# Two feed-forward up-projections computed turned: weight blocks stationary, positions moving

## The reference

```python
# block 1, hidden width 8192
y = jnp.square(jax.nn.relu(h @ w_ff1[l])) @ w_ff2[l]
# block 2, hidden width 5504
def conv_ffn(h, w_up, conv_w, conv_b, w_down):
    S = h.shape[1]
    val, gate = jnp.split(h @ w_up, 2, axis=-1)
    gp = jnp.pad(gate, ((0, 0), (CONV_W - 1, 0), (0, 0)))
    g = conv_b
    for i in range(CONV_W):                    # CONV_W = 3, causal along positions
        g = g + conv_w[i] * gp[:, i:i + S]
    return (jax.nn.silu(g) * val) @ w_down
```

## Time and profile before

| | us |
|---|---|
| median of 3 runs | 2932.68 (2930.49 to 2933.91) |
| the profiled execution, its own time | 2932.17 |
| its span | 2930.4 |
| PE busy in it | 2703.2 (92%), 12554 matmuls |
| PEld busy | 2192.0 (75%) |
| DVE busy | 1818.0 (62%) |
| ACT busy | 1224.4 (42%) |
| mean granted TensorE clock | 0.970 of full speed |

### The profile page before, as it was taken

How to read it: one execution, slowest core, us unless ns; L and a number is a source line. 1 busy time by engine, 2 the same in 40 slices (tenths; PEclk the granted TensorE clock), 3 DMA queues, 4 the chain that set the end, 5 groups by cost and what they waited for, 6 DMA issues and landing times.

```text
span 2930.4 us, 32535 instructions
## 1 busy us (share of the span) xinstructions
PE 2703.2 (92%) x12554; PEld 2192.0 (75%) x12554; DVE 1818.0 (62%) x2198; ACT 1224.4 (42%) x1560; POOL 60.8 (2%) x84
## 2 busy tenths in 40 slices
PE   4899997689799999999979999988989999999987
PEld 2378886687678888888857777776778888878876
DVE  7678677776775555555664456666455565656455
ACT  2134544333434444444444444444544434344433
POOL 1000000000000000000001000000000000000000
PEclk9899998999899999999999999999999999999999
DMA  9967895055575555555735434534345556465542
GB/s 376 335 207 271 287 315 185 29 202 197 194 287 187 186 189 188 182 188 187 253 131 194 163 130 140 179 112 172 130 171 178 196 172 199 161 200 180 165 157 100
DMA packets 154687, 562.29 MB, mean 192 GB/s; under 512 B 9672, under 2 KB 13895, under 8 KB 150736
## 3 DMA queue, kind: packets, MB, share of 16 engines
q1 hardware_dynamic: 150480, 542.15, 54.3%
q0 software_dynamic: 3920, 18.22, 1.8%
q10 hardware_dynamic: 176, 0.40, 0.0%
HBM read 556.28 MB, written 4.46 MB: 191 GB/s over the span
## 4 chain that ended last, share of the span: by engine, by line
PE 50%; issue 32%; DVE 11%; DMA 3%; ACT 3%; POOL 1%; DVEq 0%; SPq 0%; POOLq 0%; ACTq 0%
PE banks L406 15%; PE banks L408 15%; PE banks L407 15%; DMA raw_weights<-in_w_ada 3%; DVE weights_low L364 2%; ACT weights_high L351 2%; PE banks L474 1%; DVE mod_in L797 1%; PE banks L712 1%; DVE proj L1121 1%; DVE proj L994 1%; POOL small L621 1%; DVE modulation L382 1%; DVE proj L978 1%; PE banks L1676 0%
## 5 line engine op out<-in xcount | busy, mean ns | idle before, releaser
L364 DVE TENSOR_TENSOR weights_low<-raw_weights,weights_high 128x1024 fp32r<-128x1024 f32 (+2 forms) x846 | 989.5, 1178 | 913.6 <-ACT weights_high L351 892.4
L351 ACT ACTIVATE weights_high<-raw_weights 128x1024 fp32r<-128x1024 f32 (+2 forms) x846 | 857.7, 1021 | 1010.0 <-PE banks L408 955.6
L406 PE MATMUL banks<-weights_high,lhs_high 128*128 128x512 f32 (+1 forms) x2208 | 881.0, 399 | 27.8 <-DVE weights_low L364 19.9
L408 PE MATMUL banks<-weights_high,lhs_low 128*128 128x512 f32 (+1 forms) x2208 | 863.4, 391 | 0.0
L407 PE MATMUL banks<-weights_low,lhs_high 128*128 128x512 f32 (+1 forms) x2208 | 861.8, 390 | 0.0
L406 PEld LDWEIGHTS banks<-weights_high,lhs_high 128*128 128x128 f32 x2208 | 418.6, 190 | 121.7 <-DVE weights_low L364 21.5
L408 PEld LDWEIGHTS banks<-weights_high,lhs_low 128*128 128x128 f32 x2208 | 417.6, 189 | 86.6
L407 PEld LDWEIGHTS banks<-weights_low,lhs_high 128*128 128x128 f32 x2208 | 419.2, 190 | 80.8 <-issue 1.0
L406 PE MATMUL banks<-weights_high,hid_high 128*128 128x512 f32 x856 | 337.0, 394 | 16.7 <-DVE hid_low L2544 6.4
L408 PE MATMUL banks<-weights_high,hid_low 128*128 128x512 f32 x856 | 334.6, 391 | 0.0
L407 PE MATMUL banks<-weights_low,hid_high 128*128 128x512 f32 x856 | 334.6, 391 | 0.0
(11 more groups left out here) (404 smaller groups left out, 2055.3 us busy)
## 6 DMA issues: line engine op xcount, KB each, us to landing
raw_weights<-in_w_ff SPq DMA_DIRECT2D x128, 1024.0 KB, 5.0
raw_weights<-in_w_ada SPq DMA_DIRECT2D x96, 1024.0 KB, 6.6
raw_weights<-in_w_in SPq DMA_DIRECT2D x96, 1024.0 KB, 5.4
raw_weights<-in_w_up SPq DMA_DIRECT2D x80, 1024.0 KB, 4.9
raw_weights<-in_w_down SPq DMA_DIRECT2D x42, 1024.0 KB, 5.1
raw_weights<-in_w_out SPq DMA_DIRECT2D x32, 1024.0 KB, 5.2
first_weights<-in_w_in SPq DMA_DIRECT2D x16, 768.0 KB, 12.5
raw_weights<-in_w_ckv SPq DMA_DIRECT2D x8, 1024.0 KB, 4.9
```

Source lines behind the costliest of these rows:

```text
L351: act.activation(WHI[:, u % SPN, 0:c.width], RAW[:, n % RAWN, k % 2, 0:c.width], ACT.Copy).then_inc(S("high_made"), 1)
L364: dve.tensor_tensor(WLO[:, u % SPN, 0:c.width], RAW[:, n % RAWN, k % 2, 0:c.width], WHI[:, u % SPN, 0:c.width].bitcast(F32), ALU.subtract) ...
L406: nc.tensor.matmul(o, x, hi, start=(k == 0), stop=False)
L408: mm = nc.tensor.matmul(o, y, hi, start=False, stop=(k == c.kn - 1))
```

## The change

The up-projections of both feed-forward parts are made turned: for each block of 128 weight columns, the block is the stationary operand and all 256 positions of the activations are moving. The result has the hidden columns on the partitions, as the down-projection wants it. A unit of 1024 columns is 24 matmuls of 128x256 instead of 12 of 128x512, a unit of 384 columns 9 instead of 6 of 128x384, each with its own 128x128 stationary load. Two blocks share a bank. The rounds of transposes of the hidden columns are gone (`hid1`, `hid1_last`, `hid2`, `hid2_last`); ACT and DVE read the hidden columns, the gates and the values from SBUF where they read a bank. Waits on `round_ready` and `round_free` become waits on `hid_squared`, `bank_free`, `tap_done` and `unit_used`; PE waits for `hid_low2`. The number of instructions that empty banks stays (4 for each chunk of 1024 columns). Shown is the diff without context lines and small renumberings; the removed hooks of the first part stand in the functions above:

```diff
@@ -53,6 +53,7 @@
+        self.turned = out is not None and out[0].startswith("turned")
@@ -228,19 +229,21 @@
+        NATF = NAT[:, :, :].rearrange("p t n -> p (t n)")
-            return ck("w_ff1", 0, c * UW, KT, UW, second, ("relu", NAT, 0, 0), col_step=step * UW, phase=phase, ada=ada)
+            return ck("w_ff1", 0, c * UW, KT, UW, second, ("turned_relu", NATF, 0, 0), col_step=step * UW, phase=phase, ada=ada)
-        NATG, NATV = MOD[:, 0, :].rearrange("p (t n) -> p t n", t=TT), MOD[:, 1, :].rearrange("p (t n) -> p t n", t=TT)
+        NATG, NATV = MOD[:, 0, :], MOD[:, 1, :]
-            return [ck("w_up_2", 0, (1 - g) * DFF2 + c * UW, KT, w, second, ("copy", (NATG, NATV)[g], 0, 0),
+            return [ck("w_up_2", 0, (1 - g) * DFF2 + c * UW, KT, w, second, ("turned_copy", (NATG, NATV)[g], 0, 0),
@@ -391,6 +393,9 @@
+                if c.turned:
+                    pe_turned(pe, c, i, k, s)
+                    continue
@@ -412,6 +417,26 @@
+        def pe_turned(pe, c, i, k, s):
+            blocks = c.width // 128
+            for j in range(blocks):
+                b, part = divmod(j, 2)
+                if k == 0 and part == 0 and c.at["done"][b] > 0:
+                    pe.wait_ge(S(f"bank_free{b}"), val(c.at["done"][b], c.ddone[b], i))
+                x, y = (z[:, k, :] for z in c.lhs)
+                hi, lo = (w[:, s, 128 * j:128 * j + 128] for w in (WHI, WLO))
+                o = PS[:, b, T * part:T * part + T]
+                last = part == 1 or j == blocks - 1
+                nc.tensor.matmul(o, hi, x, start=(k == 0 and part == 0), stop=False)
+                nc.tensor.matmul(o, hi, y, start=False, stop=False)
+                mm = nc.tensor.matmul(o, lo, x, start=False, stop=(k == c.kn - 1 and last))
+                if last and b == c.banks - 1:
+                    mm.then_inc(S("unit_used"), 1)
+                elif last and k == c.kn - 1:
+                    mm.then_inc(S(f"bank_done{b}"), 1)
@@ -433,12 +458,19 @@
-            for b, t, h, w, count, (sem, value), col in out_banks(c, i, ("copy", "relu")):
-                kind, dst = c.at["prev"]["out"][0:2]
+            for b, t, h, w, count, (sem, value), col in out_banks(c, i, ("copy",)):
+                dst = c.at["prev"]["out"][1]
-                act.activation(o, PS[:, b, 0:w], ACT.Relu if kind == "relu" else ACT.Copy).then_inc(
+                act.activation(o, PS[:, b, 0:w], ACT.Copy).then_inc(S(f"bank_free{b}"), 1)
+            for b, _, _, _, count, (sem, value), col in out_banks(c, i, ("turned_relu", "turned_copy")):
+                kind, dst = c.at["prev"]["out"][0:2]
+                w = min(512, TT * c.at["prev"]["width"] - 512 * b)
+                if kind == "turned_relu" and id(c) in LOWS1 and b == 0:
+                    act.wait_ge(S("hid_low2"), val(LOWS1[id(c)], 4, i))
+                act.wait_ge(sem, value)
+                act.activation(dst[:, 512 * b:512 * b + w], PS[:, b, 0:w], ACT.Relu if kind == "turned_relu" else ACT.Copy).then_inc(
@@ -457,9 +489,9 @@
-            for b, t, h, w, count, _, _ in out_banks(c, i, ("relu",)):
+            for b, _, _, _, count, _, _ in out_banks(c, i, ("turned_relu",)):
-                o = NAT[:, t, 512 * h:512 * h + w]
+                o = NATF[:, 512 * b:512 * b + 512]
@@ -1748,28 +1780,26 @@
+        def hid1_parts(j, q, c, i, looped):
+            step, cs = 4 if looped else 0, slice(512 * j, 512 * j + 512)
+            hi, lo = (x[:, 2 * j:2 * j + 2, :].rearrange("p k t -> p (k t)") for x in (L2H, L2L))
+            def act_f(act):
+                if j == 0:
+                    act.wait_ge(S("unit_used"), val(c.at["u"], c.du, i))
+                act.wait_ge(S("hid_squared"), val(4 * q + j + 1, step, i))
+                act.activation(hi, NATF[:, cs], ACT.Copy).then_inc(S("hid_high2"), 1)
+            def dve_f(dve):
+                dve.wait_ge(S("hid_high2"), val(4 * q + j + 1, step, i))
+                dve.tensor_tensor(lo, NATF[:, cs], hi.bitcast(F32), ALU.subtract).then_inc(S("hid_low2"), 1)
+            return act_f, dve_f
...
+            def f(j, n):
+                return lambda eng, c, i: hid1_parts(j, HID[id(c)], c, i, i is not None)[n](eng)
+            return dict(act=[f(j, 0) for j in range(4)], dve=[f(j, 1) for j in range(4)])
@@ -1781,31 +1811,25 @@
...
+            pe.wait_ge(S("hid_low2"), val(LOWS1[id(c)], 4 if i is not None else 0, i))
+        LOWS1 = {}
...
+            LOWS1[id(c)] = 4 * (1 if n == 0 else 7)
...
+            last = next(c for _, cs in segs for c in cs if c.phase == "hid1_last")
+            def pe_wait(j):
+                return lambda pe: pe.wait_ge(S("hid_low2"), 29 + j)
+            def all_parts(n):
+                def f(eng):
+                    for j in range(4):
+                        hid1_parts(j, 7, last, None, False)[n](eng)
+                return f
+            return dict(pe=[pe_wait(k // 2) if k % 2 == 0 else None for k in range(8)], act=[all_parts(0)], dve=[all_parts(1)])
@@ -2528,56 +2553,56 @@
-            def pe_f(pe, c=None, i=None):
-                n, looped = turn_no(c, i)
-                pe_round(pe, round_of["hid2"] + 8 * n + j, NATV if j % 2 else NATG, 2 * q, nk, i, 8 if looped else 0)
+            def came(c):
+                return c if c is not None else LAST2
-                rd = round_of["hid2"] + 8 * n + j
-                act.wait_ge(S("round_free"), val(rd + 1, 8 if looped else 0, i))
+                if j % 2:
+                    if j == 1:
+                        act.wait_ge(S("unit_used"), val(came(c).at["u"], came(c).du, i))
+                    act.wait_ge(S("hid_squared"), val(32 + 4 * n + q + 1, 4 if looped else 0, i))
+                else:
+                    act.wait_ge(S("tap_done"), val(3 * (4 * n + q + 1), 12 if looped else 0, i))
-                dve.wait_ge(S("hid_high2"), val(4 * n + q + 1, 4 if looped else 0, i))
+                dve.wait_ge(S("hid_high2"), val(32 + 4 * n + q + 1, 4 if looped else 0, i))
-                rd = round_of["hid2"] + 8 * n + j
-                dve.wait_ge(S("round_ready"), val(rd + 1, 8 if looped else 0, i))
-                bank = PS[:, 4 + rd % 4, :].rearrange("p (k t) -> p k t", k=2)
+                dve.wait_ge(S(f"bank_free{q}"), val(came(c).at["done"][q], came(c).ddone[q], i))
-                        dve.wait_ge(S("hid_low2"), val(seen - 4, step, i))
+                        dve.wait_ge(S("hid_low2"), val(32 + seen - 4, step, i))
-                            src, dst = bank[:, k, 0:T - sh], GT[:, kt, sh:T]
+                            src, dst = GATES_T[:, kt, 0:T - sh], GT[:, kt, sh:T]
+                        last.then_inc(S("tap_done"), 1)
-                            last.then_inc(S("tap_done"), 1)
-                            taps = 2 * (4 * n + q) + 3 - tap
-                            dve.wait_ge(S("tap_done"), val(taps, 8 if looped else 0, i))
-                    last.then_inc(S("round_free"), 1)
+                            taps = 3 * (4 * n + q) + 3 - tap
+                            dve.wait_ge(S("tap_done"), val(taps, 12 if looped else 0, i))
-                    dve.tensor_tensor(g, g, bank[:, 0:nk, :], ALU.mult).then_inc(S("round_free"), 1)
+                    dve.tensor_tensor(g, g, VALUES_T[:, 2 * q:2 * q + nk, :], ALU.mult).then_inc(S("hid_squared"), 1)
-            return pe_f, act_f, dve_f
+            return act_f, dve_f
```

More of the change, by code:

```diff
@@ L302, in block_pair @@
         round_of, r = {}, 0
-        for nm, k in (("norm_in", 8), ("conv", 12), ("mix1", 8), ("norm_ffn1", 8), ("hid1", 28), ("hid1_last", 4), ("norm_in2", 8),
-                      ("norm_mem", 8), ("norm_cross", 8), ("cross", 2), ("norm_ffn2", 8),
-                      ("hid2", 64)):
+        for nm, k in (("norm_in", 8), ("conv", 12), ("mix1", 8), ("norm_ffn1", 8), ("norm_in2", 8),
+                      ("norm_mem", 8), ("norm_cross", 8), ("cross", 2), ("norm_ffn2", 8)):
             round_of[nm] = r
@@ L1749, in block_pair @@
                                MOD[:, 1, :], more=[clear_y])
-        def hid1_fns(nk):
[L1752 to L1772, removed]
+        def hid1_parts(j, q, c, i, looped):
[10 more added lines that the diff above has]
+            return act_f, dve_f
+        def hid1_fns(nk):
+            def f(j, n):
+                return lambda eng, c, i: hid1_parts(j, HID[id(c)], c, i, i is not None)[n](eng)
+            return dict(act=[f(j, 0) for j in range(4)], dve=[f(j, 1) for j in range(4)])
         HID, AT = {}, {}
@@ L1783, in wait_hid @@
         def wait_hid(pe, c, i):
-            r = ROUNDS_BEFORE[id(c)]
-            pe.wait_ge(S("round_free"), val(r[0], r[1] if i is not None else 0, i))
-        ROUNDS_BEFORE = {}
+            pe.wait_ge(S("hid_low2"), val(LOWS1[id(c)], 4 if i is not None else 0, i))
+        LOWS1 = {}
         waits1 = [c for _, cs in segs for c in cs if c.phase == "hid_wait" and c.w is a["w_ff2"]]
         for n, c in enumerate(waits1):
```

(21 more changed lines are left out.)

## The result

Before, 2931.59 us (median of 4 runs, 2930.30 to 2933.91); changed, **2958.51 us** (4 runs, 2956.59 to 2960.56). The ratio is 1.0093, 95% interval 1.0080 to 1.0105: slower, on the side of the forecast, but by 27 us where it said 10.

What follows compares the result with a forecast made beforehand. PE's matmul pace was taken to bound most chunks, DVE's split half of up1(0), and the chain from DVE's taps gates(2) to (4). 2932.2 + 2.1 (feed-forward 1) + 7.7 (feed-forward 2) = 2942 us; range 2912 to 2962.

Steps and rivals of the forecast that it cites:

- The pace: Chunks that PE sets: 128x256 matmuls take 120 ns each, a unit of 24 takes 2.88 us, 0.16 more than before.
- the short gap: Rival, chunks that PE sets: 256-column matmuls come at 115.6 ns, total 2917 us; chance 0.22 (extreme 111.6 ns, 2894 us: 0.04).
- the load that shows: Rival, chunks that PE sets: the constant comes on top of the load, 124.9 ns, unit 3.00, total 2973 us; chance 0.11.
- the 134 ns estimated for 256 columns: Dearer estimate for the load that shows, from the Trainium skill's gap set by load and matmul both: some 134 ns.
- a constant for each matmul: PE's fp32r matmuls: 13.3 ns on top of the columns' time, giving 106.7 + 13.3 = 120 ns for 256 columns.
- The waits that go: Feed-forward 1: PE's 3.09 us wait for the squares goes; up1(0) to 49.0 (-2.4 us), up1(1) to 46.08 (-0.6).
- the last turn: Feed-forward 1, at 1468.56 (2.78 us idle): PE goes on once the first `hid_low` ends, about 1466.75; -1.8 us.
- The chain of the gates: Feed-forward 2, gates(2) to (5): the chain stays, its taps read SBUF, -1.6 us each; gates(2) to (4) 47.1 us.
- Other costs are nil.: Whole kernel: bank emptying, SP's queue, the DMAs, ACT's new wait and POOL's later DMA add no time.
- anything else: Remaining cases, no place given, such as stalls of instruction supply at twice the rate; chance 0.06.

Runs made afterwards that it cites:

- e5: The changed kernel with only positions 0 to 127 moving (128 columns) in the turned chunks, full loads kept; 3157.71 us, one run.
- e6: The changed kernel with only 64 of each 128 weight columns stationary in the turned chunks, 256 moving columns kept; 2927.26 us, one run.
- e4: The kernel before with the four rounds of transposes in up1(1) moved three units later; 2928.17 us, ratio 0.9989.
- e7: The kernel before with late transposes in up1(1) and the loop of feed-forward 2 written out; 2921.85 us, ratio 0.9969.
- e1: The changed kernel with the loop of feed-forward 2 written out three times; 2940.81 us, ratio 1.0036 to the kernel before.

## Why the prediction was right, and where not

**The pace** was the term with most behind it and stood: 120.0 ns, units of 2.880, in both feed-forward parts. Every row of PE-bound chunks follows from it: +1.1 for each of up1(2) to (7) (46.16 or 46.17 against 46.23), +2.20 for values(0), +2.56 for values(1), -0.95 for gates(1), gates(0) +2.47 for +2.56. The rivals of the short gap and of the load that shows both fall with it. The second falls also by e5, where nothing comes on top of the load: an fp32r stream of 128 columns with a load for each matmul, of which there was no row yet, goes at 111.7 ns, and the 134 ns estimated for 256 columns did not come. But the reason given for 120, a constant for each matmul, holds only for 128 stationary columns (e6). The forecast needed no more, since its three forms all have 128.

**The waits that go**: up1(0) 48.97 (49.0 expected), up1(1) 46.08 without any wait. At the last turn I named what is late next, and it was: the four `hid_low` of DVE in the changed kernel are

```profile
1471.05 2.49 DVE L1796 TENSOR_TENSOR hid_low<-hid_rows,hid_high 128x512 fp32r<-128x512 f32 x4
```

of which the first ends near 1471.67, and PE starts at 1471.79; the half chunk ahead, transposes included, is 1.78 shorter (1.8 expected). But the same clean-up at the head of up1(1), done by e4, is worth 4.8 instead of 3.0, so most of what the turned form wins there did not need it.

**The chain of the gates** was mis-sized. "I take 0.4 for each of the four turns": the starts of DVE's taps in gates(2) of the changed kernel, and its two forms with SBUF on both sides (busy us, mean ns):

```profile
2393.64 0.73 DVE L2591 TENSOR_SCALAR modulation<-modulation,columns 128x256 f32<-128x256 f32 x2
...
2405.56 0.73 DVE L2591 TENSOR_SCALAR modulation<-modulation,columns 128x256 f32<-128x256 f32 x2
```

```profile
L2593 DVE SCALAR_TENSOR_TENSOR modulation<-modulation,columns 128x255 f32<-128x255 f32 x43 | 19.0, 481 | 2.2 <-DVE modulation L2591 1.8
...
L2591 DVE TENSOR_SCALAR modulation<-modulation,columns 128x256 f32<-128x256 f32 x43 | 15.8, 408 | 0.0
```

The period is 11.92, down by 0.26 from 12.18, just what the two TENSOR_SCALARs save that fall from 536 to 408 ns. The other taps have 481 ns from SBUF and had 478 from the bank: nothing. I had put the 413 of another operation in their place. So gates(2) to (4) gave 0.98 each and not 1.6, and gates(5) 0.45 instead of 1.6: 3.0 us too much gain in the sum.

**The step that failed is "Other costs are nil."** It went through banks, queues and buffers, but not through instruction supply. That stood only among "anything else, such as stalls of instruction supply at twice the rate", with 0.06 for all of it and no place or price. The place is the back edge of the loop over feed-forward 2 (the branch from its end to its top), taken twice; the price 12.9 us, nearly half of the whole loss: 4.1 and 4.0 standing still, then 2.8 and 2.0 for the first units after the idle time (the one of down2(1) wholly at the lower clock level). The trace of before could have raised the question: the loop's branches were plain in it, its silent instruction queue too, and the diff takes the matmuls of that body from 608 to 960. Where the limit lies it could not have told.

The sum for the profiled run, 2960.56: 2942 forecast, +12.9 branches, +3.0 gates, +1.5 in the first half of down1(7), +1.5 ahead of up1(0), in code that the change leaves alone. That is 2960.9. The 1.5 of down1(7): its first unit took 4.37 us (2.87 before) at a granted clock of 0.63, part of it at the lower level, after the 2.75 of idle. Such a slow first unit is also in the profiles of e4 (4.20) and e7 (4.17), which are not turned, and not in e1's (2.85), which is; the idle time ahead is 2.74 to 2.79 in all of them. So it is no fixed cost of the turned form; what decides it was not settled.

That 2958.51 lies inside the stated range is in part luck: its upper end, 2962, took in a part of the load's rival, which did not come, and half of "anything else"; no term of the sum stood for the stall, which is larger than the whole loss that was forecast.

## What to carry to other kernels

Halving the moving columns doubles a cost per matmul that the busy share never shows: take it from the starts of two wide forms, here 13.3 ns on 213.3 and again on 160, and multiply by the new count. Then count the instructions of every loop body that grows: beyond a limit between 800 and 960 matmuls with their loads a taken branch on PE cost 5.7 us instead of 0.2, and writing the loop out took it away. And before a form is changed to be rid of a wait, try to move the wait's cause: three units later was worth more at that place than the turning (4.8 against 3.0 us), at no cost in matmuls.

## What the hardware showed beside

- fp32r matmuls cost their columns at 2.4 GHz plus a constant: 13.3 ns with 128 stationary columns (at 512, 384 and 256 moving), 6.7 ns with 64. With 128 moving and 128 stationary columns the load is the limit, 111.7 ns.
- In e5 a continuous stream of 128x128 matmuls stood at the lower clock level for whole chunks (0.50, 213.3 ns apiece), with no idle time of PE; the changed kernel's stream of 256 columns had 1.00 in up1(1). Why was not settled.
- PE keeps a loop of 800 matmuls with their loads and fetches one of 960 again at each turn. The two branches took 5.7 us each there and 6.0 in a body of 992; with 960 smaller matmuls they took 6.1 and 5.8 in e6, 3.6 and 3.3 in e5.
